# Convolution tiles spread over the recurrent groups, mix gates moved to the end of the stage, buffers moved

## The reference

```python
h = rms_norm(x, g_mix)
z = h @ w_in + b_in
va, ga, xb, gb, sa, sb = split(z)          # 1024, 1024, 1536, 1536, 1024, 1024 channels

u = va * sigmoid(ga)
u = causal_depthwise_conv(u, conv_a_w, conv_a_b)     # 31 taps, 1024 channels
u = silu(layer_norm(u, ln_g, ln_b))                  # over the channels
y_a = u @ w_a_out

v = causal_depthwise_conv(xb, conv_b_w, conv_b_b)    # 4 taps, 1536 channels
v = rg_lru(v, w_a, b_a, w_x, b_x, lam)               # two block-diagonal gates, a scan over time
y_b = (v * gelu(gb)) @ w_b_out

m = sigmoid(sa) * y_a + sigmoid(sb) * y_b
x = x + m @ w_o
# then the feed-forward half (w_1, w_2) and the second block
```

## Time and profile before

| | us |
|---|---|
| median of 3 runs | 2653.6 |
| the profiled execution's own time | 2655.73 |
| its span, first to last instruction | 2653.9 |
| PE busy in the span | 2493.1 (94%) |
| DVE busy | 1413.2 (53%) |
| ACT busy | 810.3 (31%) |

### The profile page before, as it was taken

How to read it: one execution, slowest core, us unless ns; L and a number is a source line. 1 busy time by engine, 2 the same in 40 slices (tenths; PEclk the granted TensorE clock), 3 DMA queues, 4 the chain that set the end, 5 groups by cost and what they waited for, 6 DMA issues and landing times.

```text
span 2653.9 us, 26240 instructions
## 1 busy us (share of the span) xinstructions
PE 2493.1 (94%) x11144; PEld 2015.3 (76%) x11144; DVE 1413.2 (53%) x1699; ACT 810.3 (31%) x1202; POOL 2.8 (0%) x7
## 2 busy tenths in 40 slices
PE   8999999999999469999999999999789999999678
PEld 6686867788888148888888888887678777878577
DVE  5665665598899974243232232334665333631365
ACT  5435252512121152332022130232332231221354
POOL 0000000000000000000000000000000000000000
PEclk9999999999999789999999999999799999999889
DMA  4010202011111002211111111121111111111401
GB/s 133 27 56 27 64 12 70 20 55 48 48 48 48 16 15 61 83 49 55 48 48 48 48 48 53 46 69 40 50 46 56 38 33 48 40 48 55 128 22 59
DMA packets 224951, 133.15 MB, mean 50 GB/s; under 512 B 12730, under 2 KB 220858, under 8 KB 224834
## 3 DMA queue, kind: packets, MB, share of 16 engines
q1 hardware_dynamic: 224834, 131.47, 17.0%
HBM read 125.12 MB, written 6.32 MB: 50 GB/s over the span
## 4 chain that ended last, share of the span: by engine, by line
PE 81%; DVE 12%; ACT 4%; issue 1%; DMA 1%; SPq 1%; ACTq 0%; DVEq 0%
PE bank L535 24%; PE bank L537 24%; PE bank L536 24%; DVE uc L1559 4%; PE bank L599 4%; DVE sa L1559 2%; DVE wlo L1422 1%; PE bank L569 1%; DVE u_in L1559 1%; PE bank L770 1%; PE bank L786 1%; PE bank L678 1%; DVE uc L1676 0%; DVE tmp L1799 0%; PE bank L875 0%
## 5 line engine op out<-in xcount | busy, mean ns | idle before, releaser
L535 PE MATMUL bank<-h_hi,whi 128*128 128x512 f32 x2000 | 787.3, 394 | 3.6 <-issue 3.3
L537 PE MATMUL bank<-h_hi,wlo 128*128 128x512 f32 x2000 | 780.7, 390 | 0.0
L536 PE MATMUL bank<-h_lo,whi 128*128 128x512 f32 x2000 | 780.4, 390 | 0.0
L535 PEld LDWEIGHTS bank<-h_hi,whi 128*128 128x128 f32 x2000 | 376.7, 188 | 84.3 <-issue 5.6
L536 PEld LDWEIGHTS bank<-h_lo,whi 128*128 128x128 f32 x2000 | 376.7, 188 | 80.3 <-issue 2.9
L537 PEld LDWEIGHTS bank<-h_hi,wlo 128*128 128x128 f32 x2000 | 376.5, 188 | 78.7
L903 ACT ACTIVATE whi<-raw 128x1024 fp32r<-128x1024 f32 (+2 forms) x212 | 216.8, 1023 | 448.6 <-PE bank L537 446.6
L1422 DVE TENSOR_TENSOR wlo<-raw,whi 128x1024 fp32r<-128x1024 f32 (+2 forms) x212 | 251.4, 1186 | 163.5 <-ACT whi L903 161.8
L1559 DVE SCALAR_TENSOR_TENSOR uc<-u_in,par,uc 128x1024 f32<-128x1024 f32 x163 | 205.5, 1281 | 1.1
L537 PE MATMUL bank<-ff_hi,wlo 128*128 128x512 f32 x512 | 199.4, 389 | 0.0
L536 PE MATMUL bank<-ff_lo,whi 128*128 128x512 f32 x512 | 199.4, 389 | 0.0
(11 more groups left out here) (341 smaller groups left out, 3075.5 us busy)
## 6 DMA issues: line engine op xcount, KB each, us to landing
raw<-in_w_in SPq DMA_DIRECT2D x92, 512.0 KB, 3.6
raw<-in_w SPq DMA_DIRECT2D x64, 512.0 KB, 3.8
raw<-in_w_b_out SPq DMA_DIRECT2D x16, 384.0 KB, 3.0
raw<-in_w_out SPq DMA_DIRECT2D x11, 512.0 KB, 3.4
x_in<-in_x SPq DMA_DIRECT2D x8, 512.0 KB, 5.5
raw<-in_w_a_out SPq DMA_DIRECT2D x8, 512.0 KB, 3.8
raw<-in_w_o SPq DMA_DIRECT2D x8, 512.0 KB, 3.5
xcols<-in_x SPq DMA_DIRECT2D x16, 256.0 KB, 2.8
```

What stands on the lines that cost most here:

```text
L535: pe.matmul(target, lh, rh, start=start, stop=False, skip_group_check=True)
L536: pe.matmul(target, lh, rl, start=False, stop=False, skip_group_check=True)
L537: last = pe.matmul(target, ll, rh, start=False, stop=stop and point is not None, skip_group_check=True)
```

## The change

Five things are changed.

- **Order of the work.** The va and ga blocks of convolution tiles 2g and 2g+1 go into group g (before gate tile 0, and before the `yb` blocks); in the last group they stand after gate tiles 1 and 2. Blocks sb 0 and 1 come before the last `yb` blocks, sb 2 to 7 behind them. The sums over `uc` 0 to 5 stand before sb 7. sa 0 and 1 stand between the mean sums and the sums of squares, sa 2 to 4 behind these, and sa 5 to 7 among the `ya` blocks (list `MIX`).
- **Taps.** A tile has one accumulator (`acc0` or `acc1`), and each tap waits for the one before. `taps(n)` is called throughout the groups: 58 taps in a middle group, 248 in all.
- **DRAM.** Finished tiles 0 to 5 are written to `uc_dram` by SP (`spill`) and read back when the last group's buffers are free. A convolution tile j starts only when tile j-2 has been written.
- **Fewer instructions.** ACT makes exp of twice the exponent into the bank (two instructions of 512) in place of DVE's square of `a` (two of 512); gelu loses a DVE instruction, its constants go into ACT's scales; two `scalar_tensor_tensor` become `tensor_tensor`.
- **Homes.** The sigmoids of ga and sb stay in their PSUM banks, which DVE frees instead of ACT; the layer norm's roots and tanh lie in banks too. During the sb, sa and first ya blocks the ring has four banks. Several SBUF tiles swap regions.

```diff
         FIRST = [("xb", 0, 0), ("gb", 0, 0), ("gb", 0, 1)]
+        EARLY, STAGED = 2, 5
+        MIX = [("ya", 0), ("ya", 1), ("ya", 2), ("sa", 5), ("ya", 3), ("sa", 6), ("ya", 4), ("sa", 7), ("ya", 5), ("ya", 6), ("ya", 7)]
+        SA_AT_SQUARE, SA_AT_SILU = [11, 15], [(0, 0), (0, 4), (0, 8)]
...
 # SP
+            def spill(j):
+                ahead(number["va", j + 2] + 4)
+                w.wait_ge(*at("uc", j))
+                sp.dma_start(uc_dram[j], acc[j % 2][:]).then_inc(*landed(f"spill{j % 2}", ("spilled", j)))
             for g in range(NG):
                 load_gates(g)
-                ahead(number["yb", g, 3] + 3)
-            ahead(number["sa", DT - 1] + 3)
+                if g:
+                    spill(2 * g - 2)
+                    spill(2 * g - 1)
+                ahead(number["yb", g, 3] + 1)
...
+            for j in range(KEPT):
+                w.wait_ge(*at("spilled", j))
+                sp.dma_start(uc[j][:], uc_dram[j]).then_inc(*landed(f"uc{j}", ("reloaded", j)))
...
 # TensorE
             for g in range(NG):
                 for t in range(1 if g else 2, GT):
                     block(("gb", g, t), h, "h")
-                gate_tile(g, 0)
-                gate_tile(g, 1)
                 if g + 1 < NG:
+                    conv_blocks(2 * g)
+                    gate_tile(g, 0)
+                    gate_tile(g, 1)
                     block(("xb", g + 1, 0), h, "h")
+                    gate_tile(g, 2)
...
+                    block(("gb", g + 1, 0), h, "h")
+                    conv_blocks(2 * g + 1)
+                else:
...
+                    conv_blocks(2 * g + 1)
+                    for j in range(EARLY):
+                        block(("sb", j), h, "h")
                 for c4 in range(4):
                     add_block(("yb", g, c4), vg, f"vg{g}", GT)
...
 # ACT
+                for half in range(2):
+                    act.activation(bank("gate", g, c, 0, half)[:], T1[:, cut(half)], ACT.Exp, scale=nsp8[:, j:j + 1],
+                                   bias=nsp8[:, j:j + 1]).then_inc(*did(("a_square", j, half)))
...
                     act.activation(sq[at_sq % 4][:], uc[j][:, cut(half)], ACT.Square).then_inc(*did(("sq", j, half)))
+                    if at_sq in SA_AT_SQUARE:
+                        sa_tile(SA_AT_SQUARE.index(at_sq))
...
 # DVE
-                    b = bank("gate", g, c, 0, half)
-                    w.wait_ge(*at("a", j))
-                    dve.tensor_tensor(b[:], T2[:, cut(half)], T2[:, cut(half)], ALU.mult).then_inc(*did())
...
+                    to, weight, source = uc[j] if j >= KEPT else acc[j % 2], C("conv_a_w", m * DT + j), u_in[j % 2][:, m:m + SEQ]
+                    own()
                     if m == 0:
-                        own()
-                        dve.tensor_scalar(uc[j][:], source, weight, C("conv_a_b", j), ALU.mult, ALU.add).then_inc(*did(*point))
-                    elif m == 1 and odd is not None:
                         if j >= 2:
-                            w.wait_ge(*at("yb", NG - 1, 3, 1, 1))
-                        dve.tensor_scalar(odd, source, weight, None, ALU.mult).then_inc(*did(*point))
+                            w.wait_ge(*at("spilled", j - 2))
+                        dve.tensor_scalar(to[:], source, weight, C("conv_a_b", j), ALU.mult, ALU.add).then_inc(*did())
                     else:
-                        w.wait_ge(*now("dve_done", 0 if odd is None or m == 2 else 1))
-                        dve.scalar_tensor_tensor(to, source, weight, to, ALU.mult, ALU.add).then_inc(*did(*point))
+                        dve.scalar_tensor_tensor(to[:], source, weight, to[:], ALU.mult, ALU.add).then_inc(
+                            *did(*([("uc", j)] if m == TAPS_A - 1 else [])))
...
+                    if g == NG - 1 and c4 == 0:
+                        for j in range(EARLY):
+                            mix_gate(j)
...
+            for j in range(EARLY, DT):
+                mix_gate(j)
+                ahead(number["sb", j] + 3)
+                taps(7)
```

More of the change, by code:

```diff
@@ L197, in build_program @@
             if g + 1 < NG:
+                need_conv(2 * g)
                 for t in range(GT):
@@ L658, in tensor @@
                     sum_into(sum_banks[half], j, sq[(2 * j + half) % 4][:], ("var_sum", j, half))
+            for j in range(2, STAGED):
+                block(("sa", j), h, "h")
             for half in range(2):
@@ L663, in tensor @@
                     block_product(number["ya", j], ("ya", j, half), un, "un", half, used=half == 1)
-            for j in range(3, DT):
-                block(("ya", j), un, "un")
+            ring.names, ring.turn = ring.names + [("lnt", 0), ("lnt", 1)], 4
+            for kind, j in MIX[3:]:
+                block((kind, j), *((h, "h") if kind == "sa" else (un, "un")))
             def x1_sum(half):
@@ L1575, in yb_blocks @@
                                 dve.tensor_tensor(to, to, b[:], ALU.add).then_inc(*did(*points_))
-                            taps(2)
+                            taps(1 if c4 or half else 0)
                     ahead(number["yb", g, c4] + 3)
+                    if g == NG - 1 and c4 == 0:
+                        for j in range(EARLY):
+                            mix_gate(j)
             def conv_input(j):
+                while tap[0] <= j - 2:
+                    taps(1)
                 ahead(number["va", j] + 3)
@@ L1583, in conv_input, with mix_gate @@
                     w.wait_ge(*at("ga_tanh", j, half))
-                    dve.scalar_tensor_tensor(to, uc[j][:, cut(half)], 1.0, to, ALU.add, ALU.mult).then_inc(*did(("conv_in", j, half)))
+                    dve.scalar_tensor_tensor(to, bank("ga", j, half)[:], 1.0, to, ALU.add, ALU.mult).then_inc(
+                        *did(("conv_in", j, half), ("free", "ga", j, half)))
                 ahead(number["ga", j] + 3)
                 started[0] = j + 1
+            def mix_gate(j):
+                for half in range(2):
+                    w.wait_ge(*at("sb_tanh", j, half))
+                    dve.scalar_tensor_tensor(yb[j][:, cut(half)], bank("sb", j, half)[:], 1.0, yb[j][:, cut(half)], ALU.add,
+                                             ALU.mult).then_inc(*did(("m", j, half), ("free", "sb", j, half)))
             xb_tile(0, 0)
@@ L1641, in vector @@
-                yb_blocks(g)
-            for j in range(1, DT + 1):
-                if 2 <= j < DT:
-                    while tap[0] <= j - 2:
-                        taps(1)
-                    conv_input(j)
-                    taps(8)
-                i = j - 1
-                for half in range(2):
-                    w.wait_ge(*at("sb_tanh", i, half))
-                    dve.scalar_tensor_tensor(yb[i][:, cut(half)], sa[i][:, cut(half)], 1.0, yb[i][:, cut(half)], ALU.add,
-                                             ALU.mult).then_inc(*did(("m", i, half)))
-                ahead(number["sb", i] + 3)
-                taps(8)
-                ahead(number["sa", i] + 3)
-                taps(8)
+                    taps(8)
@@ new lines, in vector @@
+                    conv_input(2 * g)
+                    taps(2)
+                    gate_tile(g, 0)
+                    gate_tile(g, 1)
+                    xb_tile(g + 1, 0)
+                    taps(2)
+                    gate_tile(g, 2)
+                    taps(3)
+                    xb_tile(g + 1, 1)
+                    taps(3)
+                    xb_tile(g + 1, 2)
+                    taps(3)
+                    gb_tile(g + 1, 0)
+                    taps(3)
+                    conv_input(2 * g + 1)
+                else:
+                    gate_tile(g, 0)
+                    taps(2)
+                    gate_tile(g, 1)
+                    conv_input(2 * g)
+                    taps(2)
+                    gate_tile(g, 2)
+                    taps(4)
+                    conv_input(2 * g + 1)
+                    for j in range(EARLY):
+                        ahead(number["sb", j] + 3)
+                        taps(4)
@@ L1659, in vector @@
+                yb_blocks(g)
+            for j in range(EARLY, DT):
+                mix_gate(j)
+                ahead(number["sb", j] + 3)
+                taps(7)
             while tap[0] < DT:
@@ L1707, in vector @@
                         ahead(number["ya", j] + 3)
-            for j in range(3):
-                split_mix(j)
-            for j in range(3, DT):
-                ahead(number["ya", j] + 2)
-                for half in range(2):
-                    mix(j, half)
-                split_mix(j)
+            for kind, j in MIX[3:]:
+                ahead(number[kind, j] + 2)
+                if kind == "ya":
+                    for half in range(2):
+                        mix(j, half)
+                elif j == DT - 1:
+                    for i in range(5):
+                        split_mix(i)
+                if kind == "ya" and j >= 5:
+                    split_mix(j)
             for j in range(DT):
```

301 lines of the change are left out of this document (150 added, 151 removed).

## The result

The changed kernel takes 2618.9 us in the median (2616.35 to 2620.23 over 4 runs) against 2653.2 (2650.94 to 2653.69 over 4 runs) for the kernel before on the same chip. The ratio is 0.9872, with a 95% interval of 0.9860 to 0.9884: 34.3 us are gained where 41.3 were forecast. The profiled execution of the changed kernel takes 2618.1 us, 1.8 above its span of 2616.3, which is 37.6 shorter than the span before.

The account below looks back on a forecast made before the run. TensorE's waits were taken as the bound: the span of 2653.9 less 70.2 lost, plus 9.0 in middle groups and 19.9 in last group and layer norm, gives 2612.6; the forecast from the median was 2612 us, range 2599 to 2630.

Parts of the forecast that it names:

- What bounds it, and the loss before: Only TensorE's waits count; from first mean sum to first wo matmul, 70.2 of 184.7 us are lost in the old kernel.
- A middle group: TensorE stalls 2.9 us on the second va block's late weight split; three groups at 3.0 make 9.0 us.
- The bank in the last group: TensorE's fifth yb half column waits 6.8 us for sb 0's first bank, plus 1.5 for a halved clock.
- sb 1's split: Last group: the weight split of sb 1 is done at 80.0 and wanted at 78.4, costing 1.6 us.
- Tile 7: End of the sb blocks: VectorE ends the last convolution tile at 210.2, TensorE wants it at 208.6; 1.7 us.
- The layer norm: Centrings wait 2.4 us for a split; sa 2 to 4 cover first half; second half stalls 4.9, clock 1.0.
- Spills block the weights: Rival: a spill reached too early on SP's queue stops TensorE some 16 us in three groups; 2660 us, 4%.
- VectorE binds: Rival: VectorE's queue runs later than worked out, 8 us a group and 5 more at tile 7; 2632 us, 22%.
- All covered: Rival: group splits and sb banks come in time, so 9.0, 1.6, 8.3 and 1.7 us go; 2592 us, 8%.
- Table drain: Rival from the Trainium skill: each table load holds ScalarE 1.4 us longer; 2617 us, 2%.
- Free chaining: Rival from the Trainium skill: the next tap in one accumulator starts without the 0.12 us; 2605 us, 2%.
- The signs: Expected trace marks, including VectorE above 90% busy in middle groups and last mean sum about 212 us after last gb block.

Follow-up runs that it names:

- Experiment 4: Changed kernel with the weight split of the second va block ahead of the three taps behind gate tile 2 in the middle groups: 2615.5 us, ratio 0.9860.
- experiment 3: Changed kernel with the mix gates of sb 0 and 1 each directly behind their own column's yb additions: 2610.6 us, ratio 0.9842.
- experiment 10: Kernel with all edits (2588.7 us), with eight taps ahead of the tied split and none behind, instead of four and four: 2586.7 us, ratio 0.9751.
- experiment 6: Changed kernel with five instead of two taps between gate tiles 0 and 1 of the last group: 2618.3 us, ratio 0.9869.
- experiment 1: Changed kernel with the last five convolution taps ahead of the mix gate of sb 7 instead of behind it: 2606.7 us, ratio 0.9828.
- experiment 2: Changed kernel with TensorE's mean sums of six tiles behind the sb 7 block instead of in front of it: 2607.2 us, ratio 0.9827.
- experiment 7: Changed kernel with sa 2 to 4 moved from behind the square sums to in front of them: 2640.3 us, ratio 0.9950.
- experiment 8: Changed kernel with both spills of a group issued early, once the second xb block behind the va block is loaded: 2620.2 us, ratio 0.9872.
- the version with all edits: Changed kernel with the edits of experiments 1 and 3 to 6, and VectorE's two splits between the centrings moved behind the last centring: 2588.7 us, ratio 0.9759.
- experiment 5: Changed kernel with sa 4's tanh and weight split moved behind the first tile of the layer norm's second half: 2614.0 us, ratio 0.9854.

## Why the prediction was right, point by point

- **What bounds it, and the loss before.** Right: only TensorE's waits counted. 70.2 us were 68.2 by the balance above.
- **A middle group.** Place and cause right, size 9.0 us against 5.2 (3.4 on `wlo`, 1.8 on gate 2's bank). In the first group the gate chains end at T 45.8, 65.9 and 86.6 where 45.9, 66.0 and 87.2 were worked out. TensorE wants the block at T 90.5 and not 89.5, since the bank wait of 0.7 comes first, and has it at 91.9. The two waits follow one another and don't hide one another. No clock was lost behind 1.3 us. Experiment 4 shows the cause.
- **The bank in the last group.** 6.8 and 1.5 us forecast, 5.8 and 2.9 measured; experiments 3 and 10 show the cause. For this wait the reason that I gave, VectorE's backlog, was wrong (experiment 6): it comes to the additions late by what stands behind the tied split. For sb 1's split the backlog was the reason; it was late by 1.3 us as forecast (1.6), and the bank wait behind it didn't take that up, since it is as long without.
- **Tile 7.** This is the term that was mis-sized: 1.7 us forecast, 7.7 measured, 10.4 with the clock behind it. The failing words are "five full rounds and one with five taps end tile 7": they let VectorE work through. I had written of the same stretch that TensorE has ten us of mean sums "among its blocks", which puts back when TensorE wants tile 7, and didn't see that it puts back the sb 7 block that VectorE's sixth gate waits for. VectorE entered 2.3 us late, gained 1.6 us on my pace, and stood for 7.4. Experiments 1 and 2 show it.
- **The layer norm.** The squares 2.4 forecast, 2.0 measured, and 1.7 of clock at the square sums that I hadn't counted; `un_lo` 4.9 and 1.0 forecast, 3.5 and, at a clock of 1.00, nothing for it measured. That the cover by sa 2 to 4 carries the first half is right, and worth 21.4 us (experiment 7).
- **The rivals.** *Spills block the weights*: no transfer is a releaser, and by experiment 8 my price for it, 16 us a group, was wrong too: three blocks are loaded ahead, and a queue that stands for 20 to 41 us is caught up unseen. *VectorE binds*: not in a group (experiment 4). *All covered*: not so here, and reached only with the edits, 2588.7. *Table drain*: the chain times above leave no room for 1.4 us a load. In the first group a load takes 1.28 us, 121.25 to 122.53, and its root starts at 122.66. So the 2.66 us that the Trainium skill gives ("ScalarE: Activation LUTs", section "What ACT_TABLE_LOAD costs") doesn't show in this chain. *Free chaining*: seven taps in one accumulator take 9.20 us, 1.32 each, and one with a weight split behind it, 730.50 less 729.30, 1.20, so the Trainium skill's rule ("VectorE: DVE Perf Modes", section "The DRAIN you can't avoid"), by which a semaphore between them makes no difference, isn't borne out for them.
- **The sum.** Forecast 28.9 us of losses in the new order, found 34.7: tile 7 and its clock add 8.7, the square sums' clock 1.7, the middle groups take 3.8 off, the layer norm 2.8, and the yb bank and sb 1 add 0.1. That makes 32.8. The other 1.9 are no slow clock. Each wait costs TensorE 0.24 to 0.30 us beyond its idle time: at the first wait on `wlo`, at a granted 1.00, it is 1.99 us from one start (178.10) to the second after it (180.09), of which 1.29 are idle, and the 0.70 left are 0.25 more than two at the pace. The changed kernel has 14 waits in the stretch and the version with all edits, from whose busy time the loss is counted, has six. I hadn't priced this.
- **What was luck.** By the spans the forecast missed by 3.7 us (2616.3 against 2612.6). The losses were 5.8 us more than forecast and the old loss was 2.0 less than I took; 4.1 us came outside the stretch, where I had put zero, and no part of the change is shown to have brought them. Inside the 5.8, too, errors of both signs lie against each other.
- **The signs.** The last mean sums were to come 212 us after the last group's gb 2 block; they start at 218.6 (594.21 to 812.80), by tile 7. VectorE was to be above 90% busy in the middle groups and is at 77, 86 and 87% in the first three, though a group is 168.6 us long where 169.5 was worked out: its work is 146 us and not 153. That isn't what made the waits smaller. On the path to the second va block's split my chain was right to 0.7 us (T 91.7 for 92.4), and TensorE wanted the block 1.0 later. The row of the second group, columns as in the earlier trace rows:

```profile
256.55:425.10 168.55, 166.98 (x681) 127.65 (x680) 145.79 (x135) 64.30 (x76) 0.00 (x0) 1.00 0.17 49
```

## What to carry to other kernels

When one engine's queue holds both work that another engine needs and a wait for a block of that engine, work out the time of the block with everything that stands in front of it, and put the urgent work ahead of the wait: moving five instructions gave 12 us here, moving one weight split gave 5. A queue that is short of work can be late all the same, and slack made ahead of a wait on the bounding engine is waited away there (2.5 of 4.0 us in experiment 6); for what is late behind that wait, only the work behind it can be moved. Cost a single wait of TensorE of 6 to 8 us with another 2 to 3 us for its clock, any wait with another quarter of a us, and let wait and clock overlap where it then waits for a slower chain.

## What the runs showed of the hardware

- The granted clock behind a wait. For 6 us behind 5.77 us of waiting it is 0.50 (1.2 GHz) in the changed kernel: matmuls of 512 columns take 0.63 us in place of 0.39 and follow every 0.43 us in place of 0.227. For 5.6 us behind 7.75 us of waiting it is 0.52. Behind single waits of 0.74 to 1.33 us in the groups it is 1.00. Stage table of the changed kernel at the first two places, and of experiment 1 at the first:

```profile
699.55:705.55 6.00, 6.00 (x14) 4.75 (x15) 3.46 (x5) 0.00 (x0) 0.00 (x0) 0.50 0.88 314
812.80:818.40 5.60, 5.60 (x10) 3.09 (x11) 2.48 (x4) 1.69 (x3) 0.00 (x0) 0.52 0.00 0
```

```profile
700.27:706.27 6.00, 6.00 (x20) 4.81 (x21) 3.82 (x6) 0.00 (x0) 0.00 (x0) 0.74 0.89 322
```

- The clock behind one and the same wait differs between traces. Over the 6 us behind the 5.77 us, with the same instructions, it is 0.50 and 0.52 in the changed kernel and experiment 6, and 0.67 to 0.74 in experiments 1, 2, 4, 5, 7 and 8. Over the 12 us from the first of up to four waits of 0.88 us on `un_lo`, 1.85 us apart, it is 1.00 in the changed kernel and experiment 6 and 0.72 in experiments 1 to 4 and 8. Behind the same 1.97 us ahead of the last eight square sums, these took 3.70 us in experiment 1 and 5.40 in the changed kernel and in experiments 2 to 6 and 8. Each kernel has one trace, so whether the edit or the execution makes the difference isn't shown, and what decides it stays open. A microsecond or two of a forecast like this one can't be worked out from the length of the waits alone.
